# A decoder trunk on one core: values ahead of the conformer, finished rows between feed-forward pairs, attention results in a buffer of their own with the softmax steps moved

## What is computed

```python
h = rms_norm(x, mix_pre_norm[l]);  z = h @ w_in[l]            # split into pool, conformer, short-conv parts
yb = conformer_conv(za, zg, ...)                              # 31-tap depthwise convolution, layer norm, silu
y = concatenate([ya, yb, yc]) @ w_out[l];  x = x + rms_norm(y, mix_post_norm[l])
h = rms_norm(x, xattn_pre_norm[l])
y = cross_attention(h, mem_n, wq, wk, wv, wo)                 # 4 heads, 256 memory rows, softmax
x = x + rms_norm(y, xattn_post_norm[l])
h = rms_norm(x, ffn_pre_norm[l])
u = causal_dwconv(h @ w_up, w_conv);  gate, val = split(u)    # 3 taps, 2 x 2816 channels
y = (silu(gate) * val) @ w_down
x = x + rms_norm(y, ffn_post_norm[l])
```

## Time and profile before

| | us |
|---|---|
| median of 3 runs (2698.82 to 2703.56) | 2701.76 |
| the profiled execution: time, span | 2692.88, 2691.1 |
| PE busy | 2558.1 (95%) |
| DVE busy | 1579.5 (59%) |
| ACT busy | 966.0 (36%) |
| POOL busy | 977.0 (36%) |

### The profile page before, as it was taken

One profiled execution on the slowest core, in us unless ns is written; L12 is line 12 of the kernel. 1 busy time (PEld: TensorE's weight loads), 2 busy tenths in 40 slices (PEclk: granted clock), 3 DMA queues, 4 the chain that ended last, 5 costly groups with the idle time before them and its releaser, 6 DMA issues.

```text
span 2691.1 us, 33391 instructions
## 1 busy us (share of the span) xinstructions
PE 2558.1 (95%) x11713; PEld 2120.8 (79%) x11713; DVE 1579.5 (59%) x2446; ACT 966.0 (36%) x1565; POOL 977.0 (36%) x394
## 2 busy tenths in 40 slices
PE   5899899999998998999999999999999999999997
PEld 5777788878877787777888878888878888778886
DVE  4988888777736547447626456446276264562462
ACT  4233322232235444453433433333434334233332
POOL 4452400000023443334444444534444444345342
PEclk8989999999999999999999999999999999999999
DMA  7587585665834525435333244333353332443331
GB/s 245 156 295 291 191 300 182 237 255 204 312 125 172 188 82 182 159 100 184 98 109 92 83 139 151 110 93 95 88 188 95 109 94 82 133 127 108 92 94 63
DMA packets 318418, 410.59 MB, mean 153 GB/s; under 512 B 12585, under 2 KB 235070, under 8 KB 305470
## 3 DMA queue, kind: packets, MB, share of 16 engines
q1 hardware_dynamic: 309709, 396.62, 44.4%
q10 hardware_dynamic: 8560, 12.06, 1.3%
HBM read 343.62 MB, written 65.01 MB: 152 GB/s over the span
## 4 chain that ended last, share of the span: by engine, by line
PE 75%; DVE 12%; issue 6%; DMA 3%; ACT 2%; POOL 1%; SPq 0%; DVEq 0%; ACTq 0%; POOLq 0%
PE colb L1407 15%; PE colb L1408 14%; PE colb L1409 14%; PE accb L1407 10%; PE accb L1408 10%; PE accb L1409 10%; DVE arena L1143 2%; PE colb L1444 2%; DVE xh L1081 1%; POOL pair L601 1%; DVE arena L1306 1%; DVE xh L1011 1%; DVE small L1297 1%; DVE arena L1081 1%; DMA raw<-in_xattn_wq 1%
## 5 line engine op out<-in xcount | busy, mean ns | idle before, releaser
L601 POOL TENSOR_TENSOR pair<-raw,pair 128x1024 fp32r<-128x1024 f32 x387 | 976.1, 2537 | 1683.5 <-ACT pair L632 1683.1
L1407 PE MATMUL colb<-hT,pair 128*128 128x512 f32 x1952 | 766.8, 393 | 20.1 <-issue 15.0
L1408 PE MATMUL colb<-hT,pair 128*128 128x512 f32 x1952 | 763.5, 391 | 0.0
L1409 PE MATMUL colb<-hT,pair 128*128 128x512 f32 x1952 | 763.1, 391 | 0.0
L632 ACT ACTIVATE pair<-raw 128x1024 fp32r<-128x1024 f32 x387 | 405.9, 1054 | 555.1 <-PE accb L1409 316.5
L1350 DVE TENSOR_SCALAR arena<-arena,par 128x512 f32<-128x512 f32 x176 | 245.6, 1435 | 375.9 <-ACT arena L935 375.4
L1407 PE MATMUL accb<-pair,act 128*128 128x512 f32 x1120 | 440.7, 394 | 19.0 <-issue 8.0
L1407 PEld LDWEIGHTS colb<-hT,pair 128*128 128x128 f32 x1952 | 368.9, 189 | 104.1 <-issue 27.6
L1408 PE MATMUL accb<-pair,act 128*128 128x512 f32 x1120 | 437.8, 391 | 0.0
L1409 PE MATMUL accb<-pair,act 128*128 128x512 f32 x1120 | 437.7, 391 | 0.0
L1409 PEld LDWEIGHTS colb<-hT,pair 128*128 128x128 f32 x1952 | 368.7, 189 | 77.5
(11 more groups left out here) (150 smaller groups left out, 2390.0 us busy)
## 6 DMA issues: line engine op xcount, KB each, us to landing
raw<-in_ffn_w_up SPq DMA_DIRECT2D x176, 512.0 KB, 3.8
pair<-kept SPq DMA_DIRECT2D x75, 1024.0 KB, 4.9
raw<-in_ffn_w_down SPq DMA_DIRECT2D x176, 256.0 KB, 2.9
kept<-pair SPq DMA_DIRECT2D x25, 1024.0 KB, 6.1
raw<-att_a SPq DMA_DIRECT2D x64, 256.0 KB, 3.0
raw<-att_b SPq DMA_DIRECT2D x64, 256.0 KB, 5.0
raw<-in_w_in SPq DMA_DIRECT2D x17, 512.0 KB, 7.1
xh<-in_x SPq DMA_DIRECT2D x4, 2048.0 KB, 14.5
```

The costliest lines, as they stand in the source:

```text
L601: nc.gpsimd.tensor_tensor(pair[:, b, 1, :], raw[:, r, :], pair[:, b, 0, :].bitcast(F32), ALU.subtract).then_inc(lo_done, 1)
L1407: nc.tensor.matmul(dst, sh, mh, start=first, stop=False)
L1408: nc.tensor.matmul(dst, sh, ml, start=False, stop=False)
L1409: return nc.tensor.matmul(dst, sl, mh, start=False, stop=last)
```

## The change

It does four things. (1) PE computes the values right after the keys; their rounding and subtraction move ahead of the conformer on ACT and DVE, the squares of the first rows move behind the keys on ACT, and the scaling of those rows stands between values 3 and 4 on DVE. Values of heads 2 and 3 take buffers of stored keys. (2) At the end of the last ATTN tile and of FFN tiles 0 to 2, `new_rows` does the first LEAD = 3 pairs of the next feed-forward tile between its row blocks. (3) The attention result goes to `y_att`, no longer `xh`, so that the next rows are loaded earlier. (4) In attention the first probability transposes stand after score slot 6, the heads' transposes one slot earlier, `next_squares` at i = 4, and `next_rows` before the four subtractions.

```diff
-    PREP_ORDER = [("k", i) for i in range(KD)] + [("c", i) for i in range(CSLOTS)] +\
-                 [("v", i) for i in range(KD)] + [("pooled", half) for half in range(2)]
+    PREP_ORDER = [(what, i) for what in "kv" for i in range(KD)] + [("c", i) for i in range(CSLOTS)] +\
+                 [("pooled", half) for half in range(2)]
...
+        y_att = part([RB, D])
...
+            def next_attended(t):
+
+                sp.wait_ge(x_new, step_tile.at(ATTN, 0, 1))
+                sp.wait_ge(xp_full, xp.at(ATTN, t, 0))
...
+                    if p == ATTN and i == 9 and t < NT - 1:
+                        next_attended(t + 1)
...
                 key_values(0, i)
+            sc.wait_ge(xh_in, 16)
+            for r in range(RB):
+                square(xh[:, r, :], ssx[:, r:r + 1], PREP, 0, M // P + r)
+            for i in range(KD):
+                if i == 2 * HC:
+
+                    sc.wait_ge(kv_stored, 16 * HEADS)
+                key_values(1, i)
...
                     if i == 3:
                         exps(0)
-                    if i == 5:
+                    if i == 4:
+                        next_squares(ATTN, t)
+                    if i == 6:
                         for k in range(4):
                             round_item(ATTN, t, k, PROB_COL + k, act[:, 0, k, :])
-                    if i == 6:
-                        next_squares(ATTN, t)
...
             for i in range(KD):
                 key_values(0, i, KD + i)
-            ve.wait_ge(act_step, M // P + RB)
-            scale_rows(RB)
+            for i in range(KD):
+                key_values(1, i, 2 * KD + i)
+                if i == 3:
+                    ve.wait_ge(act_step, M // P + RB)
+                    scale_rows(RB)
...
+            def new_rows(p, t, y, by_row=False, between=None):
...
                 for r in range(RB):
+                    if between is not None and r:
+                        between(r - 1)
                     step(nc.vector.scalar_tensor_tensor(y[:, r, :], y[:, r, :], rs[:, r:r + 1], gain[:, :], ALU.mult, ALU.mult))
...
-                        if p == PREP and j == 1 and k % 3 == 2 and k // 3 < KD:
-                            key_values(1, k // 3, 3 * KD + 1 + k // 3)
...
                 normalise(0)
+                next_rows(ATTN, t)
                 for k in range(4):
                     lo_item(ATTN, t, k, PROB_COL + k, act[:, 1, k, :], act[:, 0, k, :])
...
-                next_rows(ATTN, t)
...
-                new_rows(ATTN, t, xh)
+                if isinstance(t, int):
+
+                    nc.vector.memset(halo[:, :, :], 0.0).then_inc(conv_ready, 1)
+                    ve.wait_ge(conv_ready, 1)
+                    new_rows(ATTN, t, y_att, between=lambda n: ffn_pair(0, n))
+                else:
+                    new_rows(ATTN, t, y_att)
...
-                    for j in range(GF):
+                    for j in range(0 if q else LEAD, GF):
+                        ffn_pair(t, q * GF + j)
...
-                new_rows(FFN, t, y_ffn, by_row=isinstance(t, int))
                 if isinstance(t, int):
-                    return
-                end()
+                    new_rows(FFN, t, y_ffn, by_row=True)
+                else:
+                    new_rows(FFN, t, y_ffn, between=lambda n: ffn_pair(t + 1, n))
+                    end()
...
                     score(i)
-                    if i == 5:
+                    if i == 6:
                         pe.wait_ge(prob_ready, probs.at(ATTN, t, RB))
```

More of the change, by code:

```diff
@@ L358, in build, with kv_chunk @@
         assert WQT + 2 == GF
+        def kv_chunk(which, h):
+            return (HEAD_KV if which and h < 2 else KV0 - 2 * which) + h
         ss = small[:, 0:8]
@@ L554, in body @@
                         sp.dma_start(gain[:, :], post_gain[p][0].partition_broadcast(P)).then_inc(gain_in, 16)
-                        if not (last and p == FFN):
+                        if p != ATTN and not (last and p == FFN):
                             sp.wait_ge(xp_full, xp.at(p, t, 0))
@@ L577, in body @@
                     store_rows(p, t, tile_of(p, t))
+                if p == MIX_LAST:
+                    next_attended(0)
             body(MIX_FIRST, 0)
@@ L582, in _ @@
             body(MIX_LAST, 0)
-            for p in (ATTN, FFN):
-                with sp.Fori(0, NT - 1) as t:
-                    body(p, t)
-                body(p, NT - 1)
+            for t in range(NT):
+                body(ATTN, t)
+            with sp.Fori(0, NT - 1) as t:
+                body(FFN, t)
+            body(FFN, NT - 1)
             sp.wait_ge(x_stored, 16 * (1 + 3 * NT - 1 + RB))
@@ L703, in _ @@
             gates(PREP, 0)
-            sc.wait_ge(kv_stored, 16 * HEADS)
-            for i in range(KD):
-                key_values(1, i)
             def stage_out(p, t, what, n):
@@ L890, in take_first @@
                 def take_first():
+                    sc.wait_ge(x_new, step_tile.at(ATTN, t, 1))
                     for r in range(RB):
@@ L1274, in _, with ffn_pair @@
             mix(MIX_LAST, 0)
+            def ffn_pair(t, n):
+                q, j = divmod(n, GF)
+                f = GF * q + j
+                u = uf[:, j % 2, :, :]
+                hs = halo.rearrange("p (g f) h -> p g f h", g=2)[:, :, f, :]
+                step(nc.vector.tensor_copy(u[:, :, 0:HS], hs))
+                freed(FFN, t, q * 2 * GF + 2 * j)
+                freed(FFN, t, q * 2 * GF + 2 * j + 1)
+                settle()
+                for k in (2, 0, 1):
+                    for e in range(2):
+                        base = par_at["ffn2"] if k == 2 else par_at["ffn01"] + k * 2 * KF
+                        w = par[:, base + f + KF * e:base + f + KF * e + 1]
+                        if k == 2:
+                            step(nc.vector.tensor_scalar(cv[:, e, :], u[:, e, k:k + T], w, None, ALU.mult))
+                        else:
+                            settle(1)
+                            step(nc.vector.scalar_tensor_tensor(cv[:, e, :], u[:, e, k:k + T], w, cv[:, e, :],
+                                                                ALU.mult, ALU.add))
+                settle()
+                nc.vector.tensor_copy(hs, u[:, :, T:LS]).then_inc(conv_ready, 1)
+                ve.wait_ge(silu_done, pairs.at(FFN, t, n) + 1)
+                nc.vector.tensor_tensor(cv[:, 1, :], cv[:, 1, :], cv[:, 0, :], ALU.mult).then_inc(y_ready, 1)
+                lo_y(FFN, t, n, act[:, 1, j, :], act[:, 0, j, :], cv[:, 1, :])
             def attn(t):
@@ L1475, in _ @@
             banks_ready(PREP, 0, item[PREP]["mem", 0], KD)
-            for i in range(KD):
-                column_slot(PREP, 0, place[PREP]["k", i], item[PREP]["k", i], memT, M)
+            for what in "kv":
+                for i in range(KD):
+                    column_slot(PREP, 0, place[PREP][what, i], item[PREP][what, i], memT, M)
             pe.wait_ge(maps_in, 16 * NW)
@@ L1489, in _ @@
             conformer(PREP, 0)
-            for i in range(KD):
-                column_slot(PREP, 0, place[PREP]["v", i], item[PREP]["v", i], memT, M)
             for half in range(2):
```

85 lines of the change are left out of this document (33 added, 52 removed).

## The result

The changed kernel takes 2739.02 us (median of 4, 2738.2 to 2742.32) against 2701.02 us before (median of 4): a ratio of 1.0146, 95% interval 1.0132 to 1.0161. Its profiled execution took 2739.5 us with a span of 2737.7 us, 46.6 us longer than the span of before.

A forecast was written before the change was run, and what follows sets the result against it. PE was taken as the bound, busy 95% of 2691.1 us, leaving some 133 us of standstills to win. Feed-forward starts +44, attention 0 and preparation 0 on the 2701.8 us median gave 2745 us, range 2708 to 2762.

The forecast's parts named there:

- +44: Whole kernel: 44 us slower, all from the four feed-forward starts, with attention and preparation at 0.
- Feed-forward starts: Four feed-forward tile starts: late x_new delays piece 10, PE 17.6 us behind each; 70.4 less 26.1 now, +44 us.
- The last term, pairs slower than PE: Feed-forward starts: five pairs to the half's end come at 11.15, not 10.88 us, another 1.4 us behind.
- Taking turns: Feed-forward starts: DVE and POOL exclude each other on their shared port, so a pair with a row block takes 13.65 us.
- sharing: Feed-forward starts: alternative reading, DVE and POOL share bandwidth; a pair about 11.3 us, x_new 5 us earlier.
- The bound from below: Feed-forward starts: shortest DVE steps, POOL never in the way; x_new at +43.4, some 8 us a start, +6 in all.
- The threshold, x_new at +41.5: Feed-forward starts: latest x_new for piece 10 in time, hi(10) by +50.9; +46.8 with a landing of 3.9 us.
- the interleave works: Rival, feed-forward starts: piece 10 in time, starts cost nothing, -26, 2676 us; 2656 with attention's -20; chance 0.1.
- Attention: Four attention tiles: first-probabilities wait replaced by 4.8 us before value slot 0; sum 0, bounds -20 and +10.
- The second wait: Attention: PE's wait for the second probabilities grows by 0.8 us, as the second half begins at 940.1, not 939.27.
- Preparation: PREP and first mixer tile: values fill PE's 7.6 us wait, taps end at 190.6, PE then waits; sum 0.
- the bounds: PREP and first mixer tile: between -9 (rows' scaling not crossed, fewer pieces) and +6 us.

The follow-up runs named there:

- e5: Changed kernel with two pairs in place of three between the row blocks (LEAD = 2): 2705.11 us, ratio 1.0030 to the kernel before.
- e2: Changed kernel with SP issuing the previous tile's store, gain and next rows behind the load of piece 13: 2693.65 us, ratio 0.9993 to the kernel before.
- e8: Changed kernel with SP's store, gain and rows behind piece 13's load, one convolution tap on ScalarE, attention's next_rows late again: 2653.30 us, ratio 0.9829.
- e1: Changed kernel without its feed-forward interleave (LEAD = 0), all else kept: 2698.53 us, ratio 1.0009 to the kernel before.
- e6: Changed kernel with one pair in place of three between the row blocks (LEAD = 1): 2695.25 us, ratio 1.0001 to the kernel before.
- e10: e8 with SP's old order, the store and its wait for x_new ahead of piece 10's load: 2695.38 us, ratio 0.9996 to the kernel before.

## Why the prediction was right, point by point

**What bounds the kernel, and the sum.** The forecast was 2745 us, from +44 on the median. Between profiled executions it was +46.6, between medians +38.0. The profiled execution of before stood 8.9 us below its median and that of the changed kernel at its median; the prediction carried the +44 over as if both stood alike. The spread of the first stages may be part of that (784.07 us is the earliest start of attention in the four traces with the values in their old place), but no run shows it. That +46.6 is so near to +44 is in part luck: the starts came 3.7 us lower than forecast, attention 4.7 us higher, and 1.6 us lie in other stretches.

**Feed-forward starts: right, 44 forecast, 40.3 measured.** In tile 1, forecast and then measured: a pair with a row block 13.65 and 13.4 us; x_new +53.5 and +52.6; piece 10 asked for at +54.1 and +53.5; landing 9.2 and 9.0 us; ready at +66.9 and +66.1; standstill at slot 10 10.3 and 10.2, at slot 9 2.1 and 1.2, none at slot 5 in both.

What this leaves out is the granted clock behind the standstill, for which the prediction had no term: slot 10 ran 1.8 us longer than 5.44 (last section). It cost nothing on top here. Slot 11 waits for piece 11, not for slot 10: PE stood 1.6 us there where 3.5 were forecast, and 1.6 + 1.8 = 3.4. The last term, pairs slower than PE, came as forecast too, at full clock; the window from slot 11 to the end of the half is

```profile
1660.13:1721.52 61.39, 61.04 (x263) 49.08 (x264) 42.96 (x56) 20.66 (x30) 27.40 (x12) 1.00 0.45 132
```

That is 61.39 us for eleven slots that take 59.84 undisturbed: 1.5 us, where 1.4 were forecast. So PE is 1.2 + 10.2 + 1.6 + 1.8 + 1.5 = 16.3 of the 16.6 us behind, where 17.6 were forecast; 0.9 of the missing 1.0 is slot 9's wait.

A pair with a row block takes 1618.73 - 1605.36 = 13.37 us, and the addition that a POOL piece crosses takes 3.42 us (L1113 above) in place of 1.21. Taking turns had given 13.65 us a pair, sharing 11.3. The Trainium skill ("SBUF — State Buffer", section "SBUF: two separate sides") calls this port pair "an exclusive lock"; the trace agrees with it.

**The bound from below, and where the interleave pays.** The threshold, x_new at +41.5, is not seen in PE's waits. In e5, with x_new at +43.0 to +45.2, PE never stands at slot 10, since slot 9 has made it late by 3.3 to 8.1 us already. ACT does wait there for piece 10 in three of the four starts:

```profile
ACT pair L653 <- DMA raw<-in_ffn_w_up: 5.1, 3, 2.4
```

In the last start, with the shortest wait at slot 9, ACT wants piece 10 at +50.5 (+50.9 in the forecast) and gets it at +52.9, 9.2 us after the issue. So x_new at +43.0 was too late by some 2 us there, which fits the threshold; no run stands just below it. With piece 10 asked for in time (e2) the rival "the interleave works" would still have been wrong: it named -26 us and e2's excess is 3 us below the kernel before. VectorE and ScalarE need 11.15 us a pair whatever stands between; e8, with shorter pairs, comes to an excess of 7.2. It was the condition of this rival, "if piece 10 is in time, the starts cost nothing", that the runs refute.

**Attention: 0 forecast, +4.7 measured, for two reasons that partly cancel.** In tiles 1 and 2 the wait that takes the place of the old one is there: 5.8 and 5.7 us by the profile's rows, 4.8 forecast. Counted from tile 1's start, 895.10 us, next_rows ends at +48.7 (48.8 forecast) and the four subtractions at +51.1 (51.6 forecast); what was off is PE, which arrives at +45.7 in place of +46.8. The second wait, forecast to grow by 0.8, is gone, but not because its work runs under the first: the second half's maxima begin at 946.12, when that wait is all but over. They and the probabilities run beside value slot 0, which the lower clock behind the wait stretches:

```profile
943.73 2.48 DVE L1044 TENSOR_TENSOR act<-colb,act 128x512 fp32r<-128x512 f32 x4
946.12 0.69 DVE L1351 TENSOR_REDUCE small<-accb 128x2 f32<-128x512 f32 x1
```
```profile
946.58:954.76 8.18, 8.18 (x24) 6.27 (x25) 7.77 (x20) 4.71 (x17) 2.39 (x1) 0.67 0.17 67
```

That slot takes 8.2 us in place of 5.44, 2.7 more, and in this the second wait is gone (1.5 us before, 2.3 with the forecast's 0.8). Sum -1.1 a tile. In the last tile the old first wait was only 2.5 us long and the new one is 6.2: +0.6. The failed step is tile 0: the prediction took all four tiles from tile 1, where `xh` has long landed. In tile 0 it lands at 824.5, so ACT stood 7.3 us ahead of its squares and PE's wait was 13.3 us where 4.8 were forecast, +6.2 for the tile. The row to read ahead would have been the issue of that load in tile 0.

**Preparation: 0 forecast, +0.4 in the two traces, -2 us by two pairs of runs.** Inside the bounds, and within what can be measured. The new order of waits was as told, with PE first at the end of the taps:

```profile
PE accb L1593 <- DVE arena L1173: 20.3, 1, 20.3
```
```profile
94.11 0.69 DVE L1146 TENSOR_TENSOR arena<-colb,arena 128x512 f32<-128x512 f32 x1 [11.52 <-PE colb L1444]
...
190.12 0.17 DVE L1173 COPY arena<-arena 128x30 f32<-128x30 f32 x1
```

The taps begin at 94.1 us (93.3 forecast), and L1173, the copy behind them, ends at 190.3 (taps and the step behind them were forecast until 190.6). What the term is worth within some 4 us stays open.

## What to carry to other kernels

Before interleaving a step into a later loop, follow the queue that waits for its last instruction: here a store on SP stood ahead of the next weight load, and that order, which the edit did not touch, cost 43 us; with the load ahead of the store the same edit is 2 to 4 us better than none. Price a wait in every tile it occurs in; the first one has its own transfers. And where two engines hand a pair back and forth, count the whole round against PE's slots: reordering work inside a round that is as long as the slots wins next to nothing (the excess of e1, e2 and e6 lies within 2.1 us), while shortening the round first makes the same reordering worth 8 to 9 us by the traces.

## What the runs showed of the hardware

The slot behind a standstill can take longer itself. The changed kernel's windows around slot 10 of tile 1: the standstill, the first 2.0 us behind it, the next 2.0, and from there to slot 11.

```profile
1641.27:1651.52 10.25, 0.16 (x1) 0.01 (x1) 1.97 (x2) 1.54 (x2) 2.34 (x1) 0.68 1.03 349
1651.52:1653.50 1.98, 1.98 (x5) 1.60 (x6) 1.98 (x5) 0.00 (x0) 0.00 (x0) 0.50 1.01 390
1653.50:1655.50 2.00, 2.00 (x7) 1.57 (x6) 1.28 (x3) 0.63 (x1) 0.00 (x0) 0.58 1.18 302
1655.50:1660.37 4.87, 3.44 (x16) 2.53 (x15) 1.91 (x4) 3.50 (x5) 2.47 (x2) 1.00 1.08 373
```

Behind 10 us without work the granted clock is 0.50, the 1.2 GHz level, and slot 10 takes 7.3 us in place of 5.44: 1.8 us that no wait shows. Shorter waits can do it too. In e2's tile 1 the slot behind a wait of 2.7 us took 7.15 us at a mean clock of 0.77; in the last feed-forward tile of the kernel before, the slot behind 2.9 us ran at 1.00. Whether the 1.8 us are lost depends on what comes next. In the changed kernel PE waits for piece 11 anyway and only waits less. In e10, with short pairs, nothing takes them up; its windows of slot 10 and of the rest of the half in tile 1:

```profile
1626.11:1634.37 8.26, 8.01 (x24) 6.34 (x24) 4.18 (x8) 4.65 (x7) 2.27 (x2) 0.64 1.09 358
1634.37:1694.33 59.96, 59.96 (x265) 49.49 (x264) 33.29 (x46) 28.17 (x44) 26.30 (x12) 1.00 0.48 141
```

Slot 10 takes 8.26 us and the eleven slots behind it 59.96, so 2.8 us are lost for good. This is why e10's starts were some 3 us above what its waits alone had let me expect. PE's longer busy time is not all the clock's either: of the 4.0 us in tile 1 of the changed kernel (123.66 against 119.68), 1.2 are the slower pairs' at full clock (61.04 us busy in the window from slot 11 on, 59.84 undisturbed).

The transfers: a load asked for directly behind the 2 MB store landed 9.0 us later, as before (9.2), and `xh` behind a store 12.3 us later. The view gives the DMA engines a busy share above 1.0 (1.03 to 1.18) over that stretch, so by it they were fully busy. e2 moves the same bytes in another order; only which of them PE waits for changed.
